# Placing the two parts of a split activation at a chosen distance from the weight ring, stage by stage

## The chip, the cores and the metric

One NeuronCore of one Trainium2 chip runs the whole program. The metric is device time in microseconds (us), the median of several executions. TensorE's two clock levels are 1.2 and 2.4 GHz; the profile gives the granted clock of each stretch as a share of 2.4 GHz.

## The reference

The input is x, 256 tokens by 1024 channels, fp32, batch 1. A first block of two layers computes, in each layer:

```python
h = rms_norm(x, norm1_g[l]);  z = h @ w_in[l]
# three mixers of slices of z: latent attention, gated linear attention, a diagonal state space
merged = g[0]*(o_a @ w_br_mla[l]) + g[1]*(o_b @ w_br_gla[l]) + g[2]*(o_c @ w_br_s5[l])
x = x + merged @ w_out[l]
h2 = rms_norm(x, norm2_g[l])
x = x + square(relu(h2 @ w_ff1[l])) @ w_ff2[l]          # 1024 -> 4096 -> 1024
```

A second block of one layer normalises, projects to q, k, v of 24 heads, to a gated convolution and to two gates, runs a banded attention and a 31-wide depthwise convolution, adds `rms_norm(merged @ w_mix_out)` to x and ends with a gated feed-forward network of hidden width 2816. All of it is fp32.

## The kernel before

Everything works on 128 partitions, with T = 256 tokens along the free dimension or, for the "down" products and the projections, as two blocks of 128 tokens. An fp32 product is split into three products in the type fp32r: `w_hi*x_hi + w_hi*x_lo + w_lo*x_hi`. The weights come in slabs of 128 x 1024 (512 KB) through rings of three: SP issues the DMA into `raw`, ScalarE (ACT) rounds it into `w_hi` (L1374, L816), GpSimd (POOL) subtracts and writes `w_lo` (L1340, L794), and TensorE (PE) waits for that. A buffer is filled again when PE has used it.

The activation has the two parts `h_hi` (rounded by ACT) and `h_lo` (the rest, by DVE), each 128 x 8 x 256 fp32r, 8192 bytes in a partition. They are two tiles allocated one behind the other; a pad `w_off` of 16 elements (64 bytes) follows, and then the rings w_hi0..2 and w_lo0..2 of 4096 bytes each. So h_lo ends 64 bytes before the ring and h_hi 64 + 8192 bytes before it. The attention's tile MD lies over the same memory.

```python
        MD = sb("MD", [P, 10240 + W_OFF], c=mid)
        mid.close()
        h_hi = sb("h_hi", [P, KD, T], f32r)
        h_lo = sb("h_lo", [P, KD, T], f32r)
        sb("w_off", [P, W_OFF])
```

The stages that use h, in order, in both layers of the first block: the input products Z (L2029 to L2031: 19 slabs, each 8 steps of three matmuls with 256 moving columns), four token-major slabs (L2075 to L2077: h is the stationary side, w moves); later the projection `merged @ w_out` (L726, 8 slabs of 12 matmuls, h stationary, 512 columns of w moving); then the feed-forward network: "up" is L2029 to L2031 again, two slabs for each 256 hidden units, "down" is L726 with c_hi and c_lo as the stationary side. PE runs up(0), then up(c+1) and down(c) by turns, so that a period of a layer is 48 up matmuls and 24 down matmuls. In the second block the same happens on L1112 to L1114 (glu, q, k, gates, convolution output, up), L1145 to L1147 (v, token-major) and L726; there a period is 96 up and 24 down matmuls. The gates of the first block are plain fp32 products of `raw` and `hN` (L2049); the branch products take `o`, `y` or `u` in the place of h, and the weights wb_hi, wb_lo for some.

The order within each engine is written out by hand, and semaphores hold it together: hh_ok and hl_ok for the parts of h, mh_ok and ml_ok for those of merged, ch_ok and cl_ok for those of the convolution, lo_done for a slab, used for the release of it.

Of the kernel before, what the change touches and what calls it, by code (L numbers as in the profile page):

```python
# [187 lines left out]
def build(nc, A, consts_dram, where, out_dram, scratch):  # L188
# [35 lines left out]
    HALF_IN = {0: 5, 2: 6, 4: 7}  # L224
    NU = U_FF + NCH
    PG_BANKS = 3
    W_OFF = 16
    PGF = 2

    ctx = ExitStack()  # L230
    with ctx:
# [12 lines left out]
        mid = ExitStack()  # L244
        MD = sb("MD", [P, 10240 + W_OFF], c=mid)
        mid.close()
        h_hi = sb("h_hi", [P, KD, T], f32r)
        h_lo = sb("h_lo", [P, KD, T], f32r)
        sb("w_off", [P, W_OFF])
        w_hi = [sb(f"w_hi{i}", [P, SLAB], f32r) for i in range(RING)]  # L250
        w_lo = [sb(f"w_lo{i}", [P, SLAB], f32r) for i in range(RING)]
        sq = sb("sq", [P, KD, T])
# [407 lines left out]
                if j % 2:  # L660
                    ins.then_inc(hf_ok.s, 1)

        def norm_lo(dve, stt, l, gain_col, gain, at=0):

            for j in range(KD):
                if j % 2 == 0:
                    dve.wait_ge(hh_ok.s, hh_ok(l, at + j // 2 + 1))
                ins = stt(h_lo[:, j, :], ps_h(j), gain_col(gain, j), h_hi[:, j, :],
                          ALU.mult, ALU.subtract)
                if j % 2:  # L670
                    ins.then_inc(hl_ok.s, 1)
# [22 lines left out]

        def merged_hi(act, A_, l, at, p):

            act.wait_ge(hf_ok.s, hf_ok(l, at + p + 1))
            A_(piece(h_hi, p), ps_piece(p), ACT.Copy).then_inc(mh_ok.s, 1)

        def merged(dve, tt, stt, l, first_slab, g, other, at, factor):  # L700

            for p in range(NP + 1):
                if p < NP:
                    dve.wait_ge(used.s, used(l, first_slab + p + 1))
                    stt(ps_piece(p), piece(g, p), 1.0, ps_piece(p), ALU.add, ALU.mult).then_inc(mg_ok.s, 1)
                    dve.wait_ge(mg_ok.s, mg_ok(l, at + p + 1))
                    stt(ps_piece(p), ps_piece(p), factor, piece(other, p), ALU.mult, ALU.add).then_inc(hf_ok.s, 1)
                if p:
                    dve.wait_ge(mh_ok.s, mh_ok(l, p))
                    tt(piece(h_lo, p - 1), ps_piece(p - 1), piece(h_hi, p - 1), ALU.subtract).then_inc(ml_ok.s, 1)  # L710
# [20 lines left out]
                last.then_inc(used.s, 1)  # L731

        def projection(pe, MM, l, weights):

            for k in range(KD - 2):
                w = weights(k)
                if k % 2 == 0:
                    pe.wait_ge(ml_ok.s, ml_ok(l, k // 2 + 1))
                by_rows(MM, l, w, h_hi, h_lo, k, k == 0, False, ps_out)
            pe.wait_ge(ml_ok.s, ml_ok(l, NP))  # L740
            for b in range(NT):
                for k in range(KD - 2, KD):
                    by_rows(MM, l, weights(k), h_hi, h_lo, k, False, k == KD - 1, ps_out, (b,))
# [53 lines left out]
        def act_second(act):  # L797
# [36 lines left out]
                              lambda i: (x_end.s, x_end(L, i + 1 - NP)) if k == 1 else (post_ok.s, i + 1))  # L834

            def h_rounded(k, gain, upto):
                prep(upto)
                for j in range(KD):
                    if j % 2 == 0:
                        act.wait_ge(ht_ps.s, ht_ps(L, NP * k + j // 2 + 1))  # L840
                    ins = A_(h_hi[:, j, :], ps_h(j), ACT.Copy, scale=col2(gain, j))
                    if j % 2:
                        ins.then_inc(hh_ok.s, 1)
# [68 lines left out]
            for n in range(16):  # L912
                w = 3 * P * (n % 2 + 1)
                if n % 4 == 0 and n:
                    take_pair(n // 4 - 1)
                act.wait_ge(pt2_ps.s, n + 1)
                A_(PT2[n % 2][:, 0:w], ps[:, PT_AT:PT_AT + w], ACT.Copy).then_inc(pt2_ok.s, 1)
                if n + 1 < 16:
                    exps(n + 1)
                if n <= 6:  # L920
                    gate(n + 1)
                if n == 2:
                    act.wait_ge(lnf_ok.s, 1)
                if n in (2, 3):
                    for j in range(4 * (n - 2), 4 * (n - 2) + 4):
                        A_(sq[:, j, :], CA[:, j, :], ACT.Tanh, scale=0.5, bias=nb2[:, 8 + j:9 + j]).then_inc(lnt_ok.s, 1)
                if n == 4:
                    act.wait_ge(lnt_ok.s, KD)
                if n in (4, 5):
                    for j in range(4 * (n - 4), 4 * (n - 4) + 4):  # L930
                        A_(CA[:, j, :], CA[:, j, :], ACT.Identity, bias=col2("b_conv_ln", j)).then_inc(lnb_ok.s, 1)
                if n == 7:
                    act.wait_ge(used.s, used(L, J_GATE + 16))
                    for p in range(NP):
                        act.wait_ge(hf_ok.s, hf_ok(L, p + 1))
                        A_(piece(h_hi, p), piece(CA, p), ACT.Copy).then_inc(ch_ok.s, 1)
                if n >= 9 and n % 2:

                    u = (n - 9) // 2
                    b = pair((V_CO + u) % 3)  # L940
                    evacuate(V_CO + u, J_CO + 2 * u + 1, [
                        (hN[:, 2 * u + i, :], b[:, i, :], ACT.Identity,
                         dict(scale=0.5, bias=col2("b_conv_out", 2 * u + i)))
                        for i in range(2)])
# [19 lines left out]
        def dve_second(dve):  # L964
# [27 lines left out]


            dve.wait_ge(cols2_ok.s, 4)
            norm_lo(dve, stt, L, col2, "g_pre_mix")

            link(V.memset(Up[:, :, 0:CONVW - 1], 0.0))
            def glu(j):
# [69 lines left out]
            for n in range(16):  # L1068
                normalise(n)
                if n + 1 < 16:  # L1070
                    if n >= 1:
                        dve.wait_ge(pt2_ps.s, n)
                    maxima(n + 1)
                if n == 1:
                    ln_scale()
                if n % 4 == 0 and n:
                    pair_lo(n // 4 - 1)
                if n == 6:
                    ln_swish()
                if n == 7:  # L1080
                    for p in range(NP):
                        dve.wait_ge(ch_ok.s, p + 1)
                        tt(piece(h_lo, p), piece(CA, p), piece(h_hi, p), ALU.subtract).then_inc(cl_ok.s, 1)
            pair_lo(3)

            g, gc = G2[:, 0:KD, :], G2[:, KD:2 * KD, :]
# [3 lines left out]
            merged(dve, tt, stt, L, J_AO, g, gc, 0, 1.0)  # L1090
            dve.wait_ge(gp_in.s, 32)
            post_norm(1)
            norm_lo(dve, stt, L, col2, "g_pre_ffn", NP)
            for c in range(NC2):
                th, gt, _ = ffb[c % 2]
                gate, up_ = pair((V_FF + 2 * c) % 3), pair((V_FF + 2 * c + 1) % 3)
# [10 lines left out]
        def pe_second(pe):  # L1107
# [29 lines left out]

            def token_major(out, w, half):


                for b in range(NT):
                    tb = slice(P * b, P * b + P)
                    for k in range(4):
                        x, first_k = 4 * half + k, half == 0 and k == 0 and b == 0
                        MM(out[:, b, :], h_hi[:, x, tb], w[0][:, k, :], start=first_k, stop=False, skip_group_check=True)  # L1145
                        MM(out[:, b, :], h_hi[:, x, tb], w[1][:, k, :], start=False, stop=False, skip_group_check=True)
                        last = MM(out[:, b, :], h_lo[:, x, tb], w[0][:, k, :], start=False,  # L1147
                                  stop=half == 1 and k == 3, skip_group_check=True)
                return last
# [6 lines left out]
            def tiles(J0, V0, lo, hi):  # L1156

                for t in range(lo, hi):
                    u = V0 + t // 2
                    if t % 2 == 0:  # L1160
                        free(u)
                    last = product(J0 + t, pair(u % 3)[:, t % 2, :], 0, h_hi, h_lo,
                                   fresh=0 if t == 0 and J0 == J_GLU else None)
                    last.then_inc(used.s, 1)

# [73 lines left out]
            def up(c):  # L1239
                for s in range(2):  # L1240
# [3 lines left out]
                    else:  # L1244
                        pe.wait_ge(ff2_ok.s, c - 1 + s)
                    for m in range(2):
                        product(up2_at(c) + 2 * s + m, pair(u % 3)[:, m, :], 0, h_hi, h_lo,
                                fresh=None if c or s or m else 1).then_inc(used.s, 1)

            up(0)  # L1250
# [96 lines left out]
        def _(act):  # L1347
# [11 lines left out]
            for l in range(DEPTH):  # L1359
# [25 lines left out]

                def h_rounded(k, gain, upto):

                    prep(upto)
                    for j in range(KD):
                        if j % 2 == 0:  # L1390
# [242 lines left out]
        def _(dve):  # L1633
# [23 lines left out]
            for l in range(DEPTH):  # L1657
# [16 lines left out]
                                     0.5, None, ALU.mult))  # L1674
                dve.wait_ge(cols_ok.s, cols_ok(l, 1))

                norm_lo(dve, stt, l, col, "norm1_g")
                dve.wait_ge(consts_all.s, 16)
                norm_h(dve, V, l, col, "norm1_g")

# [302 lines left out]
                for i in range(4):  # L1983
# [2 lines left out]
                    else:  # L1986
                        dve.wait_ge(used.s, used(l, I_OUT + KD))
                    stt(tok(xt, i), ps_out(i), 0.5, tok(xt, i), ALU.mult, ALU.add).then_inc(x_mid.s, 1)
                norm_lo(dve, stt, l, col, "norm2_g", NP)

                for c in range(NCH):
                    x = pair((U_FF + c) % PGF)
# [31 lines left out]
        def _(pe):  # L2024
# [42 lines left out]

            def token_major(out, w, half):


                for b in range(NT):
                    tb = slice(P * b, P * b + P)
                    for k in range(4):
# [9 lines left out]
            for l in range(DEPTH):  # L2083
# [25 lines left out]
                for t, (c0, n) in enumerate(Z_COLS):  # L2109
# [2 lines left out]
                    if t % 2 == 0:  # L2112
                        free(l, U_Z + t // 2)
                    out = pair((U_Z + t // 2) % PGF)[0:n, t % 2, :]
                    product(l, i, out, 0, n, h_hi, h_lo, fresh=None if t else 0).then_inc(used.s, 1)
                    if t == 11:

                        pe.wait_ge(hf_ok.s, hf_ok(l, NP))
# [280 lines left out]
                def up(c):  # L2399
                    for m in range(2):  # L2400
# [3 lines left out]
                            free(l, U_FF + c)  # L2404
                        elif m == 0:
                            pe.wait_ge(ff_sq.s, ff_sq(l, c - 1))
                        product(l, i, pair((U_FF + c) % PGF)[:, m, :], 0, P, h_hi, h_lo,
                                fresh=None if c or m else 1).then_inc(used.s, 1)

                up(0)  # L2410
# [127 lines left out]
```

## Time and profile before

| | us |
|---|---|
| median of 3 runs | 1485.75 (1484.88 to 1492.12) |
| the profiled execution | 1488.56 |
| its span | 1486.8 |
| PE busy | 1447.3 (97%) |
| PE weight loads busy | 1293.7 (87%) |
| POOL busy | 862.4 (58%) |
| DVE busy | 754.2 (51%) |
| ACT busy | 697.7 (47%) |

Busy time of PE counts matmuls that overlap in its pipeline, so the mean length of a matmul (276 ns and more) is not the time from one start to the next. A window's row gives the instructions that overlap it, so its count holds one or two at each edge that lie partly outside.

### The profile page before, as it was taken

The numbers are of one execution on the slowest core, as the hardware profiler recorded it, in microseconds if no ns is written. First come the engines' busy times: TensorE is split into PE (matmuls) and PEld (weight loads), VectorE is DVE, ScalarE is ACT, GpSimd is POOL, SyncE is SP. The second block draws the span as 40 slices with busy tenths as digits, with TensorE's granted clock in tenths as the row PEclk, the third lists the DMA queues.
The fourth block names the chain that finished last, engine by engine and source line by source line (L and its number), as shares of the span: only waits on it lengthen the run. The fifth ranks groups of instructions, "written<-read, shape, count | busy, mean of one in ns | idle before, by whom it ended". The sixth has DMA issues, their size and how long they took to land.

```text
span 1486.8 us, 24141 instructions
## 1 busy us (share of the span) xinstructions
PE 1447.3 (97%) x9839; PEld 1293.7 (87%) x9839; DVE 754.2 (51%) x1419; ACT 697.7 (47%) x1020; POOL 862.4 (58%) x364
## 2 busy tenths in 40 slices
PE   7999999999999999999999999999999999899998
PEld 7976778989999897677898889989999988799997
DVE  4978867521112697886742221229994454321112
ACT  5644225545444564422554534455445655643444
POOL 5710000878888671000087888878885536688886
PEclk9999999999999999999999999999999999999999
DMA  6632344556666563333455667656664433466664
GB/s 194 178 103 72 98 114 128 188 172 195 187 193 189 159 177 89 85 99 100 141 191 178 194 207 241 191 156 189 194 186 127 134 108 116 140 184 187 196 185 142
DMA packets 321555, 234.48 MB, mean 158 GB/s; under 512 B 9446, under 2 KB 304901, under 8 KB 321444
## 3 DMA queue, kind: packets, MB, share of 16 engines
q1 hardware_dynamic: 321444, 232.93, 53.2%
q8 instruction: 78, 1.28, 0.4%
q14 instruction: 33, 0.27, 0.1%
HBM read 231.82 MB, written 1.09 MB: 157 GB/s over the span
## 4 chain that ended last, share of the span: by engine, by line
PE 83%; issue 5%; ACT 4%; POOL 3%; DVE 3%; DMA 1%; SPq 0%; DVEq 0%; POOLq 0%; ACTq 0%
PE ps L726 19%; PE ps L2049 13%; PE ps L2029 6%; PE ps L2030 6%; PE ps L2031 6%; PE ps L1112 6%; PE ps L1113 6%; PE ps L1114 6%; POOL w_lo L1340 3%; DMA raw<-in_w_in_dram 1%; PE ps L1187 1%; PE ps L2169 1%; PE ps L2183 1%; PE ps L2150 1%; PE ps L1224 1%
## 5 line engine op out<-in xcount | busy, mean ns | idle before, releaser
L1340 POOL TENSOR_TENSOR w_lo<-raw,w_hi 128x1024 fp32r<-128x1024 f32 (+1 forms) x206 | 491.4, 2402 | 478.5 <-ACT w_hi L1374 477.9
L794 POOL TENSOR_TENSOR w_lo<-raw,w_hi 128x1024 fp32r<-128x1024 f32 x154 | 370.8, 2418 | 135.5 <-ACT w_hi L816 135.1
L1374 ACT ACTIVATE w_hi<-raw 128x1024 fp32r<-128x1024 f32 (+1 forms) x206 | 217.0, 1057 | 212.2 <-PE ps L726 90.8
L1112 PE MATMUL ps<-h_hi,w_hi 128*128 128x256 f32 x864 | 243.8, 282 | 1.7 <-POOL w_lo L794 1.0
L1113 PE MATMUL ps<-h_lo,w_hi 128*128 128x256 f32 x864 | 241.4, 279 | 0.0
L1114 PE MATMUL ps<-h_hi,w_lo 128*128 128x256 f32 x864 | 241.4, 279 | 0.0
L2029 PE MATMUL ps<-h_hi,w_hi 128*128 128x256 f32 (+1 forms) x816 | 230.4, 282 | 5.4 <-DVE h_lo L1648 3.3
L2030 PE MATMUL ps<-h_lo,w_hi 128*128 128x256 f32 (+1 forms) x816 | 228.4, 280 | 0.0
L2031 PE MATMUL ps<-h_hi,w_lo 128*128 128x256 f32 (+1 forms) x816 | 228.3, 280 | 0.0
L816 ACT ACTIVATE w_hi<-raw 128x1024 fp32r<-128x1024 f32 x154 | 161.9, 1058 | 139.0 <-PE ps L1114 61.3
L2049 PE MATMUL ps<-hN,raw 128*128 128x256 f32 x768 | 174.9, 383 | 0.0
L2049 PEld LDWEIGHTS ps<-hN,raw 128*128 128x128 f32 x768 | 143.0, 190 | 27.3 <-issue 9.1
L1112 PEld LDWEIGHTS ps<-h_hi,w_hi 128*128 128x128 f32 x864 | 163.0, 189 | 2.8 <-issue 1.4
L1114 PEld LDWEIGHTS ps<-h_hi,w_lo 128*128 128x128 f32 x864 | 163.8, 190 | 0.0
L1113 PEld LDWEIGHTS ps<-h_lo,w_hi 128*128 128x128 f32 x864 | 162.3, 188 | 0.4
L2029 PEld LDWEIGHTS ps<-h_hi,w_hi 128*128 128x128 f32 (+1 forms) x816 | 153.9, 189 | 8.7 <-POOL w_lo L1340 5.4
L2031 PEld LDWEIGHTS ps<-h_hi,w_lo 128*128 128x128 f32 (+1 forms) x816 | 155.0, 190 | 0.0
L1645 DVE TENSOR_TENSOR ps<-fr,ps 128x512 f32<-128x512 f32 (+1 forms) x36 | 24.0, 666 | 257.6 <-ACT fr L1382 257.5
L2030 PEld LDWEIGHTS ps<-h_lo,w_hi 128*128 128x128 f32 (+1 forms) x816 | 153.4, 188 | 0.9
L726 PE MATMUL ps<-w_hi,c_hi 128*128 128x512 f32 x344 | 107.1, 390 | 0.4 <-POOL w_lo L1340 0.4
L726 PE MATMUL ps<-w_lo,c_hi 128*128 128x512 f32 x344 | 107.0, 389 | 0.0
L726 PE MATMUL ps<-w_hi,c_lo 128*128 128x512 f32 x344 | 106.9, 389 | 0.0
(340 smaller groups left out, 2442.1 us busy)
## 6 DMA issues: line engine op xcount, KB each, us to landing
raw<-in_w_in_dram SPq DMA_DIRECT2D x160, 512.0 KB, 3.8
raw<-in_w_ff_dram SPq DMA_DIRECT2D x128, 512.0 KB, 4.0
raw<-in_w_ffn_in_dram SPq DMA_DIRECT2D x44, 512.0 KB, 3.8
raw<-in_w_ffn_out_dram SPq DMA_DIRECT2D x22, 512.0 KB, 3.3
raw<-in_w_out_dram SPq DMA_DIRECT2D x16, 512.0 KB, 3.2
raw<-in_w_br_gla_dram SPq DMA_DIRECT2D x8, 512.0 KB, 3.4
raw<-in_w_br_mla_dram SPq DMA_DIRECT2D x8, 512.0 KB, 4.0
raw<-in_w_br_s_dram SPq DMA_DIRECT2D x8, 512.0 KB, 3.4
```

The lines of the kernel that those rows point to most:

```text
L726: last = MM(out(2 * b + h), x[:, k, tb], y[:, 512 * h:512 * h + 512], start=first_k and n == 0, stop=last_k and n == 2, skip_group_check=True)
L794: nc.gpsimd.tensor_tensor(out=w_lo[(NS * L + i) % RING][:, 0:kt * n], in0=raw[(NS * L + i) % RING][:, 0:kt * n], in1=w_hi[(NS * L + i) % R ...
L816: A_(w_hi[(NS * L + i) % RING][:, 0:kt * n], raw[(NS * L + i) % RING][:, 0:kt * n], ACT.Copy).then_inc(hi_done.s, 1)
L1112: MM(out, w[0], x[0], start=first_k, stop=False, skip_group_check=skip)
L1113: MM(out, w[0], x[1], start=False, stop=False, skip_group_check=skip)
L1114: return MM(out, w[1], x[0], start=False, stop=last_k, skip_group_check=skip)
L1340: nc.gpsimd.tensor_tensor(out=w_lo[(NS * l + i) % RING][:, 0:kt * n], in0=raw[(NS * l + i) % RING][:, 0:kt * n], in1=w_hi[(NS * l + i) % R ...
L1374: A_(w_hi[(NS * l + i) % RING][:, 0:kt * n], raw[(NS * l + i) % RING][:, 0:kt * n], ACT.Copy)\
L2029: a = MM(out, w[0], x[0], start=first_k, stop=False, skip_group_check=skip)
L2030: MM(out, w[0], x[1], start=False, stop=False, skip_group_check=skip)
L2031: return MM(out, w[1], x[0], start=False, stop=last_k, skip_group_check=skip)
L2049: last = MM(out, w[:, k, c0:c0 + n], x[:, x0 + k, :], start=k == 0, stop=k == kt - 1)
```

## The change

h_hi and h_lo become views of one tile HR, 2 x 8192 bytes and 128 bytes more. `h_parts(stage)` places them: for distances (a, b) in bytes of the hi and the lo part, the part that lies second ends a or b bytes before the ring, the part that lies first the same and 8192 bytes further; the part with the greater distance lies first. (So with 64/128 h_lo lies first.) The pad in front of the ring grows from 64 to 128 bytes, and with it everything from the ring on moves up by 64 bytes; xt, hN and the start of MD stay. Every function that writes or reads h takes the views of its stage. The three projections and what they read (`merged_hi`, `merged`, `projection`) use `h_parts("merged")`, `token_major` those of norm1 or mix. Instructions, waits and their order stay as they are.

```diff
@@ -224,7 +224,9 @@
     PG_BANKS = 3
-    W_OFF = 16
+    W_OFF = 32
+    APART = {"norm1_0": (64, 32), "norm1_1": (80, 80), "merged": (0, 0), "norm2_0": (48, 48), "norm2_1": (64, 96),
+             "mix": (72, 72), "conv": (96, 64), "ffn": (64, 128)}
     PGF = 2
@@ -244,9 +246,14 @@
         mid.close()
-        h_hi = sb("h_hi", [P, KD, T], f32r)
-        h_lo = sb("h_lo", [P, KD, T], f32r)
-        sb("w_off", [P, W_OFF])
+        HR = sb("HR", [P, 2 * KD * T + W_OFF], f32r)
+
+        def h_parts(stage):
+            n = KD * T
+            at = [W_OFF - apart // 4 for apart in APART[stage]]
+            at = [at[0], n + at[1]] if at[0] <= at[1] else [n + at[0], at[1]]
+            return [HR[:, a:a + n].rearrange("p (k t) -> p k t", k=KD) for a in at]
+
         w_hi = [sb(f"w_hi{i}", [P, SLAB], f32r) for i in range(RING)]
@@ -660,7 +667,9 @@
-        def norm_lo(dve, stt, l, gain_col, gain, at=0):
+        def norm_lo(dve, stt, l, gain_col, gain, h, at=0):
+
+            h_hi, h_lo = h
@@ -834,6 +849,7 @@
+                h_hi, h_lo = h_parts(("mix", "ffn")[k])
@@ -933,7 +949,7 @@
-                        A_(piece(h_hi, p), piece(CA, p), ACT.Copy).then_inc(ch_ok.s, 1)
+                        A_(piece(h_parts("conv")[0], p), piece(CA, p), ACT.Copy).then_inc(ch_ok.s, 1)
@@ -992,7 +1008,7 @@
-            norm_lo(dve, stt, L, col2, "g_pre_mix")
+            norm_lo(dve, stt, L, col2, "g_pre_mix", h_parts("mix"))
@@ -1080,7 +1096,8 @@
-                        tt(piece(h_lo, p), piece(CA, p), piece(h_hi, p), ALU.subtract).then_inc(cl_ok.s, 1)
+                        c_hi_, c_lo_ = h_parts("conv")
+                        tt(piece(c_lo_, p), piece(CA, p), piece(c_hi_, p), ALU.subtract).then_inc(cl_ok.s, 1)
@@ -1090,7 +1107,7 @@
-            norm_lo(dve, stt, L, col2, "g_pre_ffn", NP)
+            norm_lo(dve, stt, L, col2, "g_pre_ffn", h_parts("ffn"), NP)
@@ -1159,7 +1176,7 @@
-                    last = product(J0 + t, pair(u % 3)[:, t % 2, :], 0, h_hi, h_lo,
+                    last = product(J0 + t, pair(u % 3)[:, t % 2, :], 0, *h_parts("conv" if J0 == J_CO else "mix"),
@@ -1244,7 +1261,7 @@
-                        product(up2_at(c) + 2 * s + m, pair(u % 3)[:, m, :], 0, h_hi, h_lo,
+                        product(up2_at(c) + 2 * s + m, pair(u % 3)[:, m, :], 0, *h_parts("ffn"),
@@ -1385,6 +1402,7 @@
+                    h_hi, h_lo = h_parts(f"norm{k + 1}_{l}")
@@ -1674,7 +1692,7 @@
-                norm_lo(dve, stt, l, col, "norm1_g")
+                norm_lo(dve, stt, l, col, "norm1_g", h_parts(f"norm1_{l}"))
@@ -1986,7 +2004,7 @@
-                norm_lo(dve, stt, l, col, "norm2_g", NP)
+                norm_lo(dve, stt, l, col, "norm2_g", h_parts(f"norm2_{l}"), NP)
@@ -2112,7 +2130,7 @@
-                    product(l, i, out, 0, n, h_hi, h_lo, fresh=None if t else 0).then_inc(used.s, 1)
+                    product(l, i, out, 0, n, *h_parts(f"norm1_{l}"), fresh=None if t else 0).then_inc(used.s, 1)
@@ -2404,7 +2422,7 @@
-                        product(l, i, pair((U_FF + c) % PGF)[:, m, :], 0, P, h_hi, h_lo,
+                        product(l, i, pair((U_FF + c) % PGF)[:, m, :], 0, P, *h_parts(f"norm2_{l}"),

```

## Rows read from the trace of the kernel before

**Rows 1.** The page's busy times.

```profile
PE 1447.3 (97%) x9839; PEld 1293.7 (87%) x9839; DVE 754.2 (51%) x1419; ACT 697.7 (47%) x1020; POOL 862.4 (58%) x364
```

**Rows 2.** The page's chain that ended last, shares by engine.

```profile
PE 83%; issue 5%; ACT 4%; POOL 3%; DVE 3%; DMA 1%; SPq 0%; DVEq 0%; POOLq 0%; ACTq 0%
```

**Rows 3.** PE's windows, feed-forward stages: window, length, busy (count), clock, DMA share, GB/s.

```profile
314.50:480.90 166.40, 166.40 (x1105) 1.00 0.62 189
795.00:964.00 169.00, 168.58 (x1117) 1.00 0.67 205
1296.50:1470.20 173.70, 173.70 (x1273) 1.00 0.61 186
```

**Rows 4.** The page's costliest groups: busy us, mean ns, idle before.

```profile
L1112 PE MATMUL ps<-h_hi,w_hi 128*128 128x256 f32 x864 | 243.8, 282 | 1.7 <-POOL w_lo L794 1.0
...
L2029 PE MATMUL ps<-h_hi,w_hi 128*128 128x256 f32 (+1 forms) x816 | 230.4, 282 | 5.4 <-DVE h_lo L1648 3.3
```

**Rows 5.** PE's windows in the second block's q and k products.

```profile
998.00:1025.00 27.00, 27.00 (x240) 1.00 0.69 197
1053.00:1092.00 39.00, 39.00 (x334) 1.00 0.65 191
```

**Rows 6.** Timeline of PE, the same stretch: first and last start of 231 steps.

```profile
998.04 0.28 PE L1112 MATMUL ps<-h_hi,w_hi 128*128 128x256 f32 x1
...
1024.22 0.28 PE L1112 MATMUL ps<-h_hi,w_hi 128*128 128x256 f32 x1
```

**Rows 7.** The chain of waits, first layer's feed-forward: start us, us, what.

```profile
336.93 5.44 PE ps L726 x24
347.83 5.46 PE ps L726 x24
...
392.22 5.44 PE ps L726 x24
403.31 5.44 PE ps L726 x24
```

**Rows 8.** The chain of waits, last feed-forward stage.

```profile
1386.54 5.44 PE ps L726 x24
1403.29 5.44 PE ps L726 x24
```

**Rows 9.** Timeline of PE, u products: first and last start of 46 steps.

```profile
260.57 0.28 PE L2030 MATMUL ps<-u_lo,wb_hi 128*128 128x256 f32 x1
...
266.08 0.28 PE L2031 MATMUL ps<-u_hi,wb_lo 128*128 128x256 f32 x1
```

**Rows 10.** Timeline of PE, y products, second layer.

```profile
758.65 0.28 PE L2029 MATMUL ps<-y_hi,w_hi 128*128 128x256 f32 x1
...
759.70 0.28 PE L2029 MATMUL ps<-y_hi,w_hi 128*128 128x256 f32 x1
```

**Rows 11.** The chain of waits, first projection.

```profile
289.42 21.99 PE ps L726 x96
```

**Rows 12.** PE by line and shape: the fp32 products on hN and on o.

```profile
L2049 PE MATMUL ps<-hN,raw 128*128 128x256 f32 x768 | 174.9, 383 | 0.0
...
L2049 PE MATMUL ps<-o,raw 128*96 128x256 f32 x96 | 22.0, 382 | 0.0
```

**Rows 13.** Who waited for whom, 1330 to 1450 us: total us, times, longest.

```profile
ACT w_hi L816 <- PE ps L1114: 32.5, 20, 1.8
...
ACT w_hi L816 <- DMA raw<-in_w_ffn_in_dram: 5.8, 3, 2.2
```

**Rows 14.** PE by line: 998 to 1025, 1053 to 1092, gates 1130.5 to 1199.6 us.

```profile
L1113 PE MATMUL ps<-h_lo,w_hi 128*128 128x256 f32 x80 | 22.1, 276 | 0.0
...
L1113 PE MATMUL ps<-h_lo,w_hi 128*128 128x256 f32 x112 | 31.5, 281 | 0.0
...
L1113 PE MATMUL ps<-h_lo,w_hi 128*128 128x256 f32 x128 | 35.7, 279 | 0.0
```

**Rows 15.** Who waited for whom, 980 to 1093 us.

```profile
ACT w_hi L816 <- DMA raw<-in_w_in_dram: 20.9, 14, 3.4
```

More of the change, by code:

```diff
@@ L695, in merged_hi @@
         def merged_hi(act, A_, l, at, p):
+            h_hi, h_lo = h_parts("merged")
             act.wait_ge(hf_ok.s, hf_ok(l, at + p + 1))
@@ L700, in merged @@
         def merged(dve, tt, stt, l, first_slab, g, other, at, factor):
+            h_hi, h_lo = h_parts("merged")
             for p in range(NP + 1):
@@ L733, in projection @@
         def projection(pe, MM, l, weights):
+            h_hi, h_lo = h_parts("merged")
             for k in range(KD - 2):
@@ L1138, in token_major @@
             def token_major(out, w, half):
+                h_hi, h_lo = h_parts("mix")
                 for b in range(NT):
@@ L2068, in token_major @@
             def token_major(out, w, half):
+                h_hi, h_lo = h_parts(f"norm1_{l}")
                 for b in range(NT):
```

## The prediction

> **What bounds the kernel now.** I read first the page's busy lines: the reader is to see that TensorE holds 97% of the span and that, its own weight loads aside, no engine passes 58% [rows 1]. The chain of waits says the same: 83% of it is matmuls [rows 2]. In the windows of the three feed-forward stages the granted clock is 1.00, which is 2.4 GHz, and the sum of gaps in PE's row is 0.4 us in 509 us [rows 3]. So there the time is the number of matmuls times the distance from one start to the next. The costliest groups are the three-term products, h_hi or h_lo moving (256 columns) over w_hi or w_lo [rows 4]: (864 + 816) x 3 = 5040 of them, to which 480 token-major ones come in which w moves and h is the stationary side. The mean of 282 ns there is the length of instructions that overlap. The cadence has to be counted from starts.
>
> That cadence has levels, and this is what the change can act on. In the second block between 998 and 1025 us, 240 records overlap a full 27.0 us; a record is 0.28 us long, so some 2.4 of the count are edges: 27.0 / 237.6 = 0.1136 us. Between 1053 and 1092 us the same lines on the same addresses give 39.0 / 331.6 = 0.1176 us [rows 5]. The first and last start of a run of 231 steps give it closer: 26.18 / 231 = 113.3 ns [rows 6]. At 2.4 GHz 256 columns are 106.7 ns, so both levels hold an excess, 6.7 and 11 ns. The feed-forward stages sit almost wholly on the upper level. In the first layer a period is 24 down matmuls (5.44 us) and 48 up matmuls: 392.22 to 403.31 is 11.09 us, hence (11.09 - 5.44) / 48 = 117.7 ns; the one period from 336.93 to 347.83 is 10.90 us, hence 113.8 ns [rows 7]. In the last stage 96 up matmuls take (1403.29 - 1386.54 - 5.44) / 96 = 117.8 ns [rows 8].
>
> **Does the distance in memory matter at all?** Summing tile sizes in the order of allocation, h and the ring of w are now 64 bytes apart modulo 512 in every stage. Other products have other distances. u over wb lies at 0: 266.08 - 260.57 = 5.51 us over 46 steps is 119.8 ns [rows 9]. y over w lies at 224: the nine steps from 758.65 to 759.70 are 1.05 us, 116.7 ns [rows 10]. With 512 moving columns, w over c lies at 0 and takes 5.44 / 24 = 226.7 ns [rows 7], w over h lies at 64 and takes 21.99 / 96 = 229.1 ns [rows 11]. So equal shapes at equal clock differ by up to 6.5 ns with the placing of the two operands, though one placing can also run at two levels. These rows also move the absolute start of the operand, so they don't separate distance from alignment.
>
> The Trainium skill speaks against the change here: "TensorE: Matmul & The Clock Gate", section "Step-by-step: what each phase is for", says that the matrix engine reads the moving operand and the weights over two independent ports, so that loading the next weights takes nothing from the running matmul. By that rule distance would be worth 0 us; the two levels and the 119.8 ns above don't agree with it as it stands, but they don't prove a port conflict either.
>
> **The change part by part.**
> 1. *Views instead of two tiles, 64 bytes more of padding.* No instruction, wait or DMA is added, removed or moved; each stage writes and reads the same number of elements. Cost 0 in count. ACT writes h_hi and DVE h_lo at other byte offsets; their groups are not where PE's gap arises. The ring, raw and everything behind move by 64 bytes. The gates' fp32 product reads hN against raw, whose distance grows from 256 to 320 modulo 512. The same line with o in place of hN has another distance and runs 382 against 383 ns [rows 12], so I take 0; bounds -0.8 and +0.8 us (1 ns on 768).
> 2. *Feed-forward stages: 48/48, 64/96 and 64/128.* If all go to the low level: first layer 13 periods of 11.09 become 5.44 + 48 x 0.1133 = 10.88, 13 x 0.21 = 2.7 us; second layer some 12 such periods, 2.5 us; last stage 11 blocks of 96, 11 x 96 x 4.5 ns = 4.7 us. Sum 9.9 us. ACT's conversions of the next weights wait there for PE (32.5 us of waiting behind the up products alone), for DMA only 5.8 us [rows 13], so a faster PE has its weights in time and the gain stays.
> 3. *Projections, merged 0/0* (w moving, h stationary): 3 x 96 matmuls from 229.1 to the 226.7 of the c products, which already lie at 0: 0.7 us. The cover is the same.
> 4. *norm1 (64/32, 80/80), mix (72/72), conv (96/64).* About a third of the steps here are low already. What is high: 1048 to 1127 us, 79 / 0.1177 = 670 matmuls; some 220 and 275 in the two norm1 stages; some 340 of the 576 in gates and conv (mean length 279 ns, between 276 at the low and 281 at the high level [rows 14]). 1500 x 4.4 ns = 6.6 us if all went low. But in the mix products ACT waits 14 times, 20.9 us, for the weights' DMA [rows 15]; a slab there at the low level takes 24 x 113.3 = 2.72 us. I take 0 of the 6.6: what one matmul gains the next weights give back, and a new distance may as well lose the low level that these stages have.
>
> The whole pool is 9.9 + 0.7 + 6.6 = 17.2 us. No row shows h at 32, 48, 72, 80, 96 or 128 bytes, so the worth of one is bounded from both sides: 17.2 us gained if every step sits at 113.3; lost, if every step takes u's 119.8: about 3750 high steps x 2.1 ns and 1700 low ones x 6.5 ns, 7.9 + 11.1 = 19 us. Between ends that far apart I take the low level for the stages of points 2 and 3: it is the level nearest to them that a run of theirs already shows [rows 7], and at the present distance the upper level is one that the cadence settles in for good [rows 8], so another distance has more to give than to take there. Sum: 9.9 + 0.7 = 10.6 us gained.
>
> The profiled execution took 1488.56 us (span 1486.8 and 1.8 around it), so 1478.0 for it; it lies 2.8 us above the median of the runs, 1485.75, from which the same sum gives **1475.1 us**.
>
> **The rivals.**
> - *Nothing moves* (the skill's rule on ports does this). The two levels run at identical addresses [rows 5], so the level may be set by the phase in which PE takes up a stage and not by the distance. Then the new kernel has the same mix of levels: 1485 us, within 3. Against it: 119.8 and 116.7 ns at other distances. A weaker form: one feed-forward stage gains, another stays or a norm1 stage loses; gain 3 to 6 us, 1481.
> - *All stages reach the low level, or a lower one.* 1485.75 - 17.2 = 1468.5. For it: nothing but the chosen value of point 4. Against it: the DMA waits [rows 15]. The skill's "Wait — 56ns, not 53.3ns?" on the same page gives 2.5 ns over the column count as the floor; at an estimated 109.2 ns per 256 columns some 20 us more would go, which no row of 256 fp32r columns shows.
> - *Slower: the new distances settle on a higher level.* Place: norm1 and mix, whose low third is lost, and the up products at 48 and 128 bytes. Price: half of the 19 us above, 9.5 us, 1495. It decides from the point where the mean over all 5520 steps lies above 116.3 ns, today's mean by the sum above (113.3 + 3750 x 4.4 / 5520). For it: u's level, the highest, is one the same engine settles in for 46 steps on end; and the sum rests on offsets of 48, 72 and 80 that are no multiple of 64, as the starts of u and y aren't.
> - *It doesn't do what it says.* The helper places h_hi and h_lo so that the second part ends the stated bytes before the ring and the first 8192 bytes further; I find no stage whose writer and readers name different stages, so this is given nothing of its own.
>
> **How the numbers follow.** Forecast 0.45; all low or lower 0.08; nothing moves 0.25 and its weaker form 0.08; slower 0.14. What a measurement of this kernel can tell from no change is about 0.5%, 7.4 us. Faster by over that: 0.45 + 0.08 = 0.53. Within: 0.33. Slower: 0.14. The likeliest case's own range is 1471 to 1479. The given range reaches down to beyond the full pool (1464) and up into the slower case (1492): outside it I leave about 0.04 below and 0.10 above.
>
> **What would show it.** Right: in the chain of waits the first layer's periods from one 24-fold down group to the next at 10.88 to 10.90 instead of 11.09, the last stage's at 16.32 instead of 16.75; the mean of the h_lo lines in those stages at 276 instead of 280 and 281; a projection of 96 in 21.76 instead of 21.99. Rival one: periods unchanged. Slower: means of 283 and weight loads of 192 ns. Point 4: the number of records in 27 us of the mix products stays near 240 and DMA waits don't shrink. I am wrong altogether if the up products gain nothing and the time falls in another place, or if the levels differ between executions of the same kernel.

## The result and the profile after

The changed kernel takes 1498.84 us (median of 4 executions, 1497.47 to 1501.24) against 1487.03 for the kernel before on the same chip: ratio 1.0078, 95% interval 1.0059 to 1.0097. It is 11.8 us slower. 1475.1 had been forecast, and the range ended at 1492.

The page of the changed kernel: PE is busy for 12.4 us more, POOL, ACT and DVE within 3 us of before [rows 1]; the chain of waits has 87% of matmuls, from 83% [rows 2].

```profile
span 1497.7 us, 24141 instructions
...
PE 1459.7 (97%) x9839; PEld 1306.4 (87%) x9839; DVE 756.9 (51%) x1419; ACT 697.8 (47%) x1020; POOL 861.3 (58%) x364
...
PE 87%; issue 4%; ACT 3%; POOL 3%; DVE 2%; DMA 1%; SPq 0%; DVEq 0%; POOLq 0%; ACTq 0%
...
L1129 PE MATMUL ps<-HR,w_hi 128*128 128x256 f32 x864 | 246.2, 285 | 1.4 <-DVE HR L993 1.3
...
L2047 PE MATMUL ps<-HR,w_hi 128*128 128x256 f32 (+1 forms) x816 | 232.4, 285 | 5.1 <-DVE HR L1666 3.6
...
L2067 PE MATMUL ps<-hN,raw 128*128 128x256 f32 x768 | 174.9, 383 | 0.0
```

The instruction counts are the same. The products on h have grown from a mean of 282 to 285 ns [rows 4]; the fp32 products on hN, whose distance from raw also changed, are at 383 ns to the digit [rows 12]. So the loss is in the cadence of the h products, that is in the time from the start of one matmul to the start of the next, and the chain of waits shows it in the feed-forward stages. First the first layer (start, length, what), where a period was 11.09 us [rows 7]:

```profile
404.63 5.45 PE ps L739 x24
415.81 5.45 PE ps L739 x24
```

11.18 us: (11.18 - 5.45) / 48 = 119.4 ns a step. Then the last stage, where it was 16.75 us [rows 8]:

```profile
1397.00 5.44 PE ps L739 x24
1413.85 5.44 PE ps L739 x24
```

16.85 us: (16.85 - 5.44) / 96 = 118.9 ns. Nothing here reached the 10.88 and 16.32 us that were forecast. The q and k products, PE's windows (window, length, busy and count, clock, DMA share, GB/s):

```profile
1000.00:1027.00 27.00, 27.00 (x227) 1.00 0.68 195
1060.00:1099.00 39.00, 39.00 (x327) 1.00 0.65 188
```

With 2.4 records taken off for the edges, 27.0 / 224.6 = 120.2 ns and 39.0 / 324.6 = 120.1 ns, where the kernel before had 113.6 and then 117.6 [rows 5]. The level of 113.3 ns is gone there and the upper one is higher. Only the projections gained, 21.99 to 21.78 us [rows 11]:

```profile
289.73 21.78 PE ps L739 x96
```

The table counts every stage from the starts of its matmuls in the two traces: the time from the first to the last start, and the mean step with the gaps over 135 ns left out (for the projections 512 columns, gaps over 245 ns left out). "Low" is the number of steps under 115.5 ns, of which the level of 113.3 ns consists.

| stage | distances after | us before | us after | ns before (low) | ns after (low) |
|---|---|---|---|---|---|
| norm1 Z, layer 0 | 64/32 | 57.2 | 58.5 | 114.9 (290) | 118.8 (71) |
| norm1 Z, layer 1 | 80/80 | 56.3 | 57.7 | 115.2 (265) | 119.1 (8) |
| feed-forward, layer 0 | 48/48 | 177.1 | 178.8 | 117.1 (121) | 119.2 (97) |
| feed-forward, layer 1 | 64/96 | 179.5 | 180.1 | 116.8 (167) | 117.8 (21) |
| glu, q, k | 72/72 | 112.4 | 115.6 | 115.3 (547) | 120.0 (1) |
| gates | 72/72 | 69.0 | 70.2 | 115.7 (174) | 119.8 (2) |
| convolution output | 96/64 | 41.7 | 43.6 | 115.9 (76) | 118.0 (17) |
| last feed-forward | 64/128 | 184.3 | 185.4 | 117.8 (4) | 118.8 (55) |
| three projections | 0/0 | 65.5 | 64.7 | 229.1 | 227.1 |

A count of low steps doesn't by itself mean the low level. In the kernel before, nearly all low steps come in runs, up to 284 in a row at 113 to 114 ns (the longest in glu, q and k). In this trace of the changed kernel no two of them follow each other in any stage: they are single steps of a pattern that repeats, at 48/48 for instance 119, 115, 119, 118, 118, 120, 124, 121 ns and again from the front, whose mean is 119 ns.

The token-major stages move by under 0.3 us. The nine lines sum to +11.6 us, beside 11.8 in the medians and 10.9 in the two spans. Of the 1.9 us of the convolution output 1.5 have nothing to do with distance. Fourteen of its steps, from 1216.05 us on, are 207 to 214 ns long, and the granted clock of that stretch is 0.53 in the mean, near its lower level of 1.2 GHz; TensorE had waited 1.16 us for DVE just before. No DMA moved anything in it, so it is no wait for weights. The first line is that stretch; the second is the same stretch in another execution of the changed kernel (below), where the steps are 118 ns and the stage takes 42.1 us:

```profile
1216.05:1219.20 3.15, 3.15 (x17) 0.53 0.00 0
1215.40:1218.40 3.00, 3.00 (x27) 1.00 0.00 0
```

Without these 1.5 us the nine lines sum to +10.1 us. Over the 5430 steps of the full clock the mean went from 116.4 to 118.9 ns: +13.4 us. With the clock's 1.5 us more and 0.7 us less in the projections that would be 14.2; the 2.6 us between this and 11.6 are, by difference, waits that the slower pace covers.

### The profile page after: what moved, and what is told of

The parts are those of the page before. It is cut to its first block, busy times and chain, and to the rows that moved or that the text cites. A ratio compares the mean times of both kernels' runs of the same rounds, so it can differ in the third digit from the quotient of the medians.

```text
span 1497.7 us, 24141 instructions
## 1 busy us (share of the span) xinstructions
PE 1459.7 (97%) x9839; PEld 1306.4 (87%) x9839; DVE 756.9 (51%) x1419; ACT 697.8 (47%) x1020; POOL 861.3 (58%) x364
## 4 chain that ended last, share of the span: by engine, by line
PE 87%; issue 4%; ACT 3%; POOL 3%; DVE 2%; DMA 1%; SPq 0%; DVEq 0%; POOLq 0%; ACTq 0%
PE ps L739 19%; PE ps L2067 13%; PE ps L1129 7%; PE ps L1130 7%; PE ps L1131 7%; PE ps L2047 7%; PE ps L2049 6%; PE ps L2048 6%; POOL w_lo L1357 3%; PE ps L1204 1%; PE ps L1241 1%; PE ps L2187 1%; PE ps L2201 1%; PE ps L2168 1%; DMA raw<-in_w_in_dram 1%
## 5 line engine op out<-in xcount | busy, mean ns | idle before, releaser
L1129 PE MATMUL ps<-HR,w_hi 128*128 128x256 f32 x864 | 246.2, 285 | 1.4 <-DVE HR L993 1.3
L1130 PE MATMUL ps<-HR,w_hi 128*128 128x256 f32 x864 | 244.4, 283 | 0.0
L1131 PE MATMUL ps<-HR,w_lo 128*128 128x256 f32 x864 | 243.9, 282 | 0.0
L2047 PE MATMUL ps<-HR,w_hi 128*128 128x256 f32 (+1 forms) x816 | 232.4, 285 | 5.1 <-DVE HR L1666 3.6
L2048 PE MATMUL ps<-HR,w_hi 128*128 128x256 f32 (+1 forms) x816 | 230.4, 282 | 0.0
L2049 PE MATMUL ps<-HR,w_lo 128*128 128x256 f32 (+1 forms) x816 | 229.8, 282 | 0.0
L1129 PEld LDWEIGHTS ps<-HR,w_hi 128*128 128x128 f32 x864 | 163.7, 189 | 2.3 <-issue 1.9
L1130 PEld LDWEIGHTS ps<-HR,w_hi 128*128 128x128 f32 x864 | 164.4, 190 | 0.4
L1131 PEld LDWEIGHTS ps<-HR,w_lo 128*128 128x128 f32 x864 | 163.4, 189 | 0.0
L2047 PEld LDWEIGHTS ps<-HR,w_hi 128*128 128x128 f32 (+1 forms) x816 | 153.8, 188 | 8.7 <-POOL w_lo L1357 4.9
L2048 PEld LDWEIGHTS ps<-HR,w_hi 128*128 128x128 f32 (+1 forms) x816 | 154.1, 189 | 0.9
L2049 PEld LDWEIGHTS ps<-HR,w_lo 128*128 128x128 f32 (+1 forms) x816 | 154.6, 190 | 0.0
```

Source lines behind the costliest of these rows:

```text
L1129: MM(out, w[0], x[0], start=first_k, stop=False, skip_group_check=skip)
L1130: MM(out, w[0], x[1], start=False, stop=False, skip_group_check=skip)
L1131: return MM(out, w[1], x[0], start=False, stop=last_k, skip_group_check=skip)
L2047: a = MM(out, w[0], x[0], start=first_k, stop=False, skip_group_check=skip)
L2048: MM(out, w[0], x[1], start=False, stop=False, skip_group_check=skip)
L2049: return MM(out, w[1], x[0], start=False, stop=last_k, skip_group_check=skip)
```

## Experiments

All kernels below start from the changed one. Only distances, pads or tile places are edited. Means of steps are counted as in the table, from one traced execution of each kernel.

**All stages back at 64/64, the ring still 64 bytes higher.**

```diff
-    APART = {"norm1_0": (64, 32), "norm1_1": (80, 80), "merged": (0, 0), ...
+    APART = {"norm1_0": (64, 64), "norm1_1": (64, 64), "merged": (64, 64), ...   # all eight 64/64
```

> All eight stages at 64/64, as before, but ring, h and all behind the ring still 64 bytes higher than before. Theory A (only the distance between moving operand and weights counts): the settled cadences of before return, up products 117.7 ns in the feed-forward stages and 113.3 for part of norm1 and mix; time 1487 within 3 us. Theory B (the start addresses count, so the shift of 64 bytes made the loss): cadences as in the changed kernel, mix near 120.0 ns, time 1496 or more.

Measured: ratio to the kernel before 1.0004 (0.9992 to 1.0017), median 1488.4 of 10 executions. The cadences are back: first layer's up 116.8 ns with 169 low, glu, q, k 115.6 ns with 480 low, mean over all h steps 116.4 ns. The last stage, by its chain of waits:

```profile
1387.46 5.44 PE ps L738 x24
1404.21 5.44 PE ps L738 x24
```

16.75 us, as in [rows 8]. So the views, the 64 bytes more of padding and the shifted start addresses cost nothing that can be measured; what was lost came with the distances.

**The same with the projections at 0/0.**

```diff
-    ... "merged": (64, 64) ...
+    ... "merged": (0, 0) ...
```

> As the run at 64/64 everywhere, but the three projections at 0/0. Theory A: the projections take 21.55 to 21.6 us instead of 21.75 (226.9 against 229.1 ns a matmul), 0.7 us in all, all else as before; 1486. Theory B: the same 0.7 us below the 64/64 run, at 1495.

Measured: ratio 0.9990 (0.9977 to 1.0003). The projections took 21.59, 21.82 and 21.57 us against 21.75, 21.76 and 21.76 at 64/64, 227.2 ns a matmul against 229.0. The effect is there in the step, and 0.3 us is all that it brings in this pair (0.8 between the two kernels compared above); in the whole time it can't be told from nothing.

**The changed kernel a second time, unedited.**

> The changed kernel once more. If distance sets the cadence that a stage settles in, the means per stage repeat within 0.3 ns: mix 120.0, first layer's up 119.2, second layer's up 117.8, last up 118.8. If the level is an accident of the phase in each execution, they come out differently, by 2 ns or more in some stage.

Measured: 1497.70 us. Mean steps 118.8, 119.2, 119.0, 117.8, 120.0, 119.9, 118.0 and 118.8 ns in the order of the table, each within 0.2 of the first trace. The convolution output took 42.1 us in place of 43.6, at the full clock from its start. At the changed distances the cadence repeats from one execution to the next. At 64/64 it need not (see the hand-over below).

**Each stage at another distance.**

```diff
+    APART = {"norm1_0": (0, 0), "norm1_1": (128, 128), "merged": (32, 32), "norm2_0": (32, 32),
+             "norm2_1": (0, 0), "mix": (64, 0), "conv": (0, 64), "ffn": (128, 128)}
```

> Each stage read by its own cadence: norm1 of layer 0 at 0/0, of layer 1 at 128/128, projections 32/32, layer 0 feed-forward 32/32, layer 1 feed-forward 0/0, mix 64/0, conv 0/64, last feed-forward 128/128. Theory A1 (multiples of 64 are good, others bad): 0/0 and 128/128 give 113.3 or 117.7 ns, 32/32 gives 119 or more. Theory A2 (distance 0 is where weights and moving data collide, as u over wb at 119.8): 0/0 gives 119.8, 128/128 117.7 or less, 32/32 between. If the cadence does not depend on distance: 113.3 and 117.7 mixed everywhere.

Measured: 1501.93 us in one execution. 0/0 gives 119.8 ns in both stages that had it, 128/128 gives 119.0 and 119.7, 32/32 118.3, 64/0 and 0/64 117.8 and 117.9. The projections at 32/32 are the worst seen, 233.2 ns; their row of 21.99 us at 64/64 [rows 11] has become

```profile
291.62 22.38 PE ps L738 x96
```

A2 held for 0/0 and failed for 128/128, which is no better than 0. A1 failed: 0 and 128 are multiples of 64 and bad. With one part at 64 and the other at 0 the mean is that of the upper level, but by another pattern (115 to 122 ns where the upper level has 117 to 119), and the level of 113.3 is lost. This run also separates distance from alignment, which the prediction's rows could not: at 128/128 both parts of h start on the same bytes as in the kernel before and only the ring has moved, and the last feed-forward stage goes from 117.8 to 119.7 ns; with ring and h both moved by 64 bytes (the first experiment) nothing changed.

**Four and eight bytes off 64.**

```diff
+    APART = {"norm1_0": (60, 60), "norm1_1": (68, 68), "merged": (16, 16), "norm2_0": (68, 68),
+             "norm2_1": (60, 60), "mix": (56, 56), "conv": (68, 68), "ffn": (60, 60)}
```

> Distances 4 and 8 bytes off 64: norm1 60/60 and 68/68, layer 0 feed-forward 68/68, layer 1 60/60, mix 56/56, conv 68/68, last feed-forward 60/60, projections 16/16. Theory A (the cadence depends on the distance, best at 64 and worse with each step off it, since 72 gave 120.0, 80 gave 119.1 and 48 gave 119.2): 60 and 68 lose the low level of 113.3 and settle at 117.7 to 119; mix at 56 gives 120.0 as 72 did. Rival (only steps of 16 or 32 bytes matter to the memory): 60 and 68 read as 64, 113.3 in part and 117.7.

Measured: 1505.83 us in one execution. 60/60 is the slowest of all, 121.7 to 121.8 ns in three stages; 68/68 gives 118.1 to 118.8, 56/56 120.1. The last feed-forward stage at 60/60:

```profile
1401.85 5.46 PE ps L738 x24
1418.99 5.46 PE ps L738 x24
```

(17.14 - 5.46) / 96 = 121.7 ns, against 117.8 at 64/64 [rows 8]. The rival, that small steps don't matter, is out: four bytes to either side of 64 are enough to lose both of its levels. That 60 would be worse than 56 nobody expected.

**Far distances.**

```diff
-    W_OFF = 32
+    W_OFF = 80
+    APART = {"norm1_0": (192, 192), "norm1_1": (320, 320), "merged": (128, 128), "norm2_0": (192, 192),
+             "norm2_1": (320, 320), "mix": (192, 192), "conv": (320, 320), "ffn": (256, 256)}
```

> The pad before the ring at 320 bytes; norm1 of layer 0, layer 0 feed-forward and mix at 192/192, norm1 of layer 1, layer 1 feed-forward and conv at 320/320, projections 128/128, last feed-forward 256/256. If the distance counts modulo 128 (two 64-byte halves taken in turns), 192 and 320 behave as 64: 113.3 in part, else 117.7, and 256 as 0: 119.8 to 120.0; projections at 128 as at 0: 226.7. If it counts as such: 192 and 320 differ from 64 and from each other.

Measured: 1493.50 us in one execution. 320/320 behaves as 64/64: 115.7 ns in norm1 (219 low), 116.8 in the feed-forward of layer 1 (164 low). 192/192 has the same two levels, 283 and 272 cycles in the mean of a slab, with fewer low: 116.1 in norm1 (166 low), 117.8 in glu, q, k and layer 0's up (5 and 3 low). 256/256 is as 0/0, 119.9 ns. So for the up products the levels of 64 come back at 192 and 320, and the cadence of 0 at 256, as a period of 128 bytes would have it; between these multiples of 64 no second period was tried. The projections don't: at 128 they take 232.3 ns, at 0 227.1. That half of the expectation failed.

**Only the mix stage back at 64/64.**

```diff
-             "mix": (72, 72), "conv": (96, 64), "ffn": (64, 128)}
+             "mix": (64, 64), "conv": (96, 64), "ffn": (64, 128)}
```

> The changed kernel with the mix stage alone (glu, q, k, v, gates) put back from 72/72 to 64/64; all other distances as changed. If the loss of the mix stage is its distance, glu, q and k take 112.4 to 113.7 us instead of 115.6 and the gates 69.0 instead of 70.2: 3.2 to 4.4 us less, time 1494, ratio to before 1.005. If the time was lost through something else that moved with the stages, the time stays at 1498.

Measured: ratio 1.0038 (1.0023 to 1.0052), median 1494.09. glu, q and k took 113.6 us and the gates 68.8, together 3.5 us less than in the changed kernel. The window of q and k:

```profile
1000.00:1027.00 27.00, 27.00 (x232) 1.00 0.68 194
```

27.0 / 229.6 = 117.6 ns in place of 120.2, all of it on the upper level: 4 low steps of 960. With this stage at the same distance, the kernel at 64/64 throughout had 480 low there. So 72/72 costs 2.0 us in glu, q and k even against the upper level of 64/64, and which of its two levels a stage at 64/64 gets, distance doesn't say.

**Another hand-over: c_hi and c_lo at 64.** The down products stand between the up products, so their length may set the phase in which these begin. c_hi and c_lo lie at 0 from the ring; moved by 64 bytes they cost the down products something.

```diff
-        sb("c_off", [P, 56], c=ffn)
+        sb("c_off", [P, 40], c=ffn)      # h at 64/64, projections 0/0
```

> All stages at 64/64, projections 0/0, and the tiles c_hi and c_lo of the down products 64 bytes lower, so that they lie at 64 instead of 0 from the ring. The down products then take 229.0 instead of 226.7 ns: 1032 x 2.3 = 2.4 us more. Theory P (the phase with which the down products hand over to the up products picks the level of 113.3 or 117.7): the up products of the last stage leave 117.7 and go low for some periods, up to 4.7 us less there and 5 us less in the layers. Rival (each address pair goes to 117.7 by itself): up stays 117.7, the time is 2.4 us above the same kernel with c at 0, 1489 to 1490.

> h at 64/64, projections 0/0, both c at 64, now timed: last stage's up products at 113.6 as in the single look (997 of 1056 low), 2.4 us lost in the down products; 1485, ratio 0.998, at most 0.999.

Measured: 1485.18 us in the first run, one execution; in the second, 1483.04 us against 1488.00 for the kernel before, ratio 0.9963 (0.9949 to 0.9978). The last stage by its chain of waits and by line:

```profile
1383.00 5.49 PE ps L738 x24
1399.40 5.49 PE ps L738 x24
```

```profile
L1129 PE MATMUL ps<-HR,w_hi 128*128 128x256 f32 x352 | 97.3, 276 | 0.0
...
L738 PE MATMUL ps<-w_hi,c_lo 128*128 128x512 f32 x72 | 22.4, 393 | 0.0
```

16.40 us in place of 16.75: (16.40 - 5.49) / 96 = 113.6 ns, 993 of 1056 steps low, against 4 before. The mean length is 276 ns, that of the low level [rows 14]. In the layers 640 and 567 of 768 are low. The down products pay 228.8 to 229.5 ns where they took 226.8 to 227.2. h's addresses relative to the ring are those of the kernel before; only what runs in front of the up products has changed.

The two runs are executions of one and the same kernel, and they don't agree in every stage. The feed-forward stages repeat (997 and 993 low steps in the last). But glu, q and k have 237 low steps (116.7 ns) in the first and 8 (117.8 ns) in the second, and norm1 of layer 0 has 91 (116.9 ns) and 299 (114.9 ns). So at 64/64 the level of a stage can differ between executions of one kernel, by 2 ns in the mean of norm1.

**One of the two c parts at 64.**

```diff
 (a) c_hi at 0, c_lo at 64
         c_hi = sb("c_hi", [P, 4, T], f32r, c=ffn)
+        sb("c_gap", [P, 16], c=ffn)
         c_lo = sb("c_lo", [P, 4, T], f32r, c=ffn)
 (b) c_hi at 64, c_lo at 0: the same gap, and
-        sb("c_off", [P, 56], c=ffn)
+        sb("c_off", [P, 40], c=ffn)
```

(a): 

> h at 64/64, projections 0/0, c_hi left at 0 and c_lo alone at 64 from the ring. The third of the down products that load c_lo may take 229 instead of 226.7 ns, 344 x 2.3 = 0.8 us. Theory P (the hand-over from the down products, whose last two load c_lo, picks the level of the up products): the last stage's up products go low, -3.9 us there, some -1 in layer 0; total 1484, ratio 0.9975. Rival (all down products must be at 64 for that): up stays at 117.7, 1488.

(b): 

> The mirror of it: c_hi at 64, c_lo at 0. Down: 688 x 2.3 = 1.6 us more. Theory P: the last two down products lie at 0 as before, so the up products stay at 117.7 ns; 1489. Rival: any change in the down products' length shifts the phase, and the level of the up products changes here too, in either direction.

Measured: (a) ratio 0.9970 (0.9959 to 0.9982), 1005 of 1056 low in the last stage; the down products took 231.1 ns, more than with both parts at 64: some 4.3 us over the 1032 of them (against 226.9 ns before), where 0.8 us in all had been expected. The gap puts c_lo 64 bytes to the other side than in the runs above; whether that is the reason no run shows. (b) 0.9963 (0.9949 to 0.9977), 755 of 1056 low, and 723 and 603 of 768 in the layers. So the narrow form of the theory, that the last two down products decide, fell with (b): each of the three changes in the down products that were tried moved most of the up products to the low level, where in three kernels with c at 0 the last stage had 2 to 4 low steps.

**The changed kernel with c at 64.**

```diff
-        sb("c_off", [P, 56], c=ffn)
+        sb("c_off", [P, 40], c=ffn)      # all distances of h as changed
```

> The changed kernel with both c at 64. Theory D (the new distances have no low level at all): up products stay at 118 to 119 ns in all three feed-forward stages whatever the phase, low steps under 10% of them, down products 2.4 us longer, 1500. Rival (the change only met a bad phase): the last stage's up products (64/128) go to 113 to 114 as they do at 64/64 with this c, and the time falls to 1494 or less.

Measured: 1499.67 us in one execution. Up products 119.2, 117.8 and 118.8 ns, as in the changed kernel to 0.2, with 98, 39 and 62 low steps; down products 229.3 ns.

```profile
1396.81 5.50 PE ps L738 x24
1413.71 5.50 PE ps L738 x24
```

(16.90 - 5.50) / 96 = 118.8 ns. The hand-over that brings 993 of 1056 low at 64/64 brings 62 at 64/128. The rival, that the change only met a bad phase, is out for this hand-over, the one other that was tried with the new distances: the low level didn't come back. Nor do the up products have more than two low steps in a row at any distance tried but 64, 192 and 320; at the last two the runs are up to 142 and 122 long.

## Why the prediction was wrong

*Bound and cadence.* Right: PE's cadence is the time of these stages, it has levels at equal addresses, and distance matters. The rule of the Trainium skill cited there ("TensorE: Matmul & The Clock Gate", section "Step-by-step: what each phase is for"), that weights and moving operand come over independent ports and don't disturb each other, leaves distance no effect; the means of 113.6 to 121.8 ns at equal shape and clock don't agree with it. What in the memory or in the array is shared no run shows.

*Step 1, views, pad and shift at 0 us.* Right: 1.0004 with all distances at 64.

*Step 2, the feed-forward stages.* This is the step that failed: "I take the low level for the stages of points 2 and 3", worth 9.9 us. They lost 1.8, 0.6 and 1.0 us. The value was taken as "the level nearest to them that a run of theirs already shows" - but the row that showed it was a row at 64/64 [rows 7]; it said nothing on 48, 96 or 128. The argument that a stage stuck on the upper level "has more to give than to take" treated the two levels as those of the memory in general. They belong to the distance of 64 and were found again only at 192 and 320: every other distance tried for both parts of h settled between 118.1 and 121.8 ns, and with one part at 64 none was under 117.7.

*Step 3, projections.* Right in mechanism: 0.7 us was forecast, from 229.1 to 226.7 ns a matmul; the step went from 229.1 to 227.1, which is 0.6 us, and the rest of the 0.8 us between the two profiles lies in the gaps.

*Step 4, norm1, mix and conv at 0 us.* Wrong in sign. That "a new distance may as well lose the low level" was written down and then given no price. The same paragraph says that about a third of the steps there are low already; that is the share over all stages, and here it was about half (its own count has 1500 high ones, of some 2900). The loss was 1.3 + 1.4 in norm1, 3.2 + 1.3 in mix and 0.4 in conv beside its stretch at the lower clock, 7.6 us of the 10.1 that remain without that stretch: here the kernel before had its low steps, 1352 of its 1667. The waits of ACT for the weights' DMA, which had been the reason to take 0, fell in mix from 20.9 [rows 15] to 10.2 us at the slower pace.

```profile
ACT w_hi L831 <- DMA raw<-in_w_in_dram: 10.2, 5, 2.5
```

*The rivals.* What happened is the third, with its places (norm1, mix, and the up products at 48 and 128 bytes) and nearly its price, 9.5 forecast, 11.8 measured in the medians; it had the chance 0.14. That the price came so near is in part luck, since it was half of a bound. Its point of decision, a mean of 116.3 ns, agrees with 116.4 before and 118.9 after. "Nothing moves" was half of the truth: something other than distance decides between the two levels of 64, but at the new distances there is no level of 113.3 to be had. The prediction's last sign of being wrong altogether, levels that differ between executions of the same kernel, did come up, at 64/64 (237 against 8 low steps in glu, q and k); at the changed distances it did not, and the loss is far larger than what such a difference makes. Two signs stood in the rows and were weighed too low. u over wb at 119.8 ns [rows 9] and y at 116.7 [rows 10] were both worse than the low level, and no row at any distance but 64 had it. The nine steps of y were also only one of two values: over the whole stage y over w, at 224, has 116.7 ns in layer 1 and 117.8 ns in layer 0 of the kernel before, so that at this distance too the addresses don't fix the mean.

## What to carry to other kernels

When a trace shows two levels of one instruction at the same addresses, trace the same kernel a second time to see which stages repeat, and then vary what runs just in front. Here that gave 0.37% (1483.0 us, ratio 0.9963; the two kernels with one c part moved, at 0.9970 and 0.9963, can't be told from it), where none of the distances tried for the up products gained. A favourable setting that is already in place is a sample of one: rows taken at it don't price its neighbours, and a low level found only at the present setting is something to lose. Read such a change by the step of each stage in one profile before asking the total: in two executions of the changed kernel it repeated within 0.2 ns. And look at the granted clock before calling a longer stage a wait.

## What was not expected of the hardware

For fp32r products with 256 columns moving and fresh weights for each, the step in ns by the distance in bytes from the moving operand to the ring, both parts alike: 0: 119.8; 32: 118.3; 48: 119.2; 56: 120.1; 60: 121.7; 64: 113.3 or 117.7; 68: 118.1 to 118.8; 72: 120.0; 80: 119.1; 128: 119.0 to 119.7; 192 and 320: 113.3 or 117.7; 256: 119.9. In these multiples of 64 it repeats with 128 bytes, and a move of four bytes changes it. y over w at 224, which lies at 96 within such a period and was never tried for both parts of h, has 116.7 or 117.8 ns. The token-major products (256 columns of w moving, h stationary) have two levels too: at 64/64 those of layer 1 took 117.8 ns in the kernel before and 113.3 in the first experiment, and v took 117.8 ns at 64 and at 72 but 113.4 at 192. With 512 columns of w moving and h stationary another order holds: 0: 227.1; 16: 228.4; 64: 229.0; 128: 232.3; 32: 233.2. The low step is 272 cycles at 2.4 GHz, 16 over the column count, and the mean of no stage came below it. Which of the two levels a stage takes at 64/64 isn't fixed by addresses. In the feed-forward stages the work just ahead moves it (4 low steps before, 993 with c at 64). The same glu, q and k products had 547, 480, 316 and 4 low steps of 960 in four kernels that differ from each other elsewhere, but also 237 and 8 in two executions of one kernel, so these four numbers can't be put down to the kernels. What fixes it stays open.
